# A decoder trunk in split fp32: the products with the weights' remainders moved to the end of each slab

## The chip, the cores and the metric

One Trainium2 chip, one core. The metric is the device time of one launch in microseconds (us). The core has TensorE (PE in the profile; its weight loads are PEld), VectorE (DVE), ScalarE (ACT), GpSimd (POOL) and the queue SP, which here starts the weight transfers.

## What is computed

The reference is one inference step of a two-layer hybrid decoder with 256 prompt tokens and 32 sample tokens (8 sequences of 4). All 288 tokens go through the kernel together.

```python
for l in range(DEPTH):                       # DEPTH = 2, D_MODEL = 2048, D_FF = 5632
    h = rms_norm(x, norm_mix[l])
    proj = h @ w_in[l]                       # 5120 columns
    q, k, v, hq, hf, hi, hg, cb, cc, ch = jnp.split(proj, split_idx, axis=-1)
    a = attention with sinks over a window of 128      # 16 query heads, 4 kv heads
    o = hgrn2_mixer(hq, hf, hi, hg, S0, lb, g_norm)    # 4 heads of 128
    yc = short_conv(cc * ch, buf, conv_w[l])
    x = x + jnp.concatenate([a, o, cb * yc], axis=-1) @ w_out[l]
    h = rms_norm(x, norm_ffn[l])
    gate, up = jnp.split(h @ w_gate_up[l], 2, axis=-1)
    x = x + (jax.nn.silu(gate) * up) @ w_down[l]
y = rms_norm(x, norm_final)
```

New caches and states are outputs too.

## The kernel before

Activations lie with the model dimension on the 128 partitions and the 288 tokens along the free axis. The five large matrices of a layer are one stream of slabs. A slab has 4 chunks of 128 input rows by 256 output columns (512 KB), and a layer has 376 slabs: 80 for the input projection, 16 and 16 for the two halves of the output projection, and for the feed-forward, in two parts of 24 and 20 tiles of its inner width, 96 and 48, then 80 and 40. Two layers have 752 slabs.

Every large product is done in fp32r three times, for accuracy: the weights are split into a rounded part `whi` and a remainder `wlo`, the activations into `xh` and `xl` (or `ah`/`al`, `mh`/`ml`, `fh`/`fl`). The sum has `whi*xh`, `whi*xl` and `wlo*xh`. A slab thus has 4 chunks x 2 column halves x 3 = 24 products of 128x128 by 128x288, each with its own weight load.

The engines work as a line, each on its own program, tied by semaphores:

- SP loads slab n into `raw` (ring of 4, L370) once the remainder of the slab four before is done.
- ScalarE rounds it, `whi <- raw` (L399), and counts `hi_ready`. It waits for `slab_used`, that is until TensorE is done with the slab four before.
- VectorE subtracts, `wlo = raw - whi` (L675), and counts `lo_ready`.
- TensorE (`group`, L1388) waits for `lo_ready`, does the 24 products and counts `slab_used` on the last.

ScalarE and VectorE call `hi` and `lo` two slabs ahead (`LEAD = 2`) of the slab that TensorE is to be at, in program order with their other work. The slabs of one pair of output tiles form a group (4 slabs in the projections into the layer, 2 in each half of the output projection, 6 or 5 in the down projection). Two pairs of PSUM banks alternate between groups. At a group's end VectorE empties the banks: `out_proj` (L707), `out_add` into `x` (L715), or `gb`/`fa` in the feed-forward (L1055, L1061), and counts `group_out`, for which TensorE waits before it uses the banks again.

In the second half of the output projection (`half_b`, a loop of 4 x 2 groups) each group also prepares the next norm's input. After `out_add` ScalarE makes `xh` (`scale_hi`, L406), then VectorE `xl` (`scale_lo`, L694), and GpSimd adds squares. After the first feed-forward group TensorE makes the mean square (L1437, L1438), ScalarE the root (L412), VectorE the reciprocal (L700), and only then VectorE can write `gb` and ScalarE its sigmoid (L572); ScalarE's next `whi` stands behind it. At the very start of the program ScalarE squares `x` between its first `whi` (L601), in step with GpSimd's sums (L1332).

The mixers' small products are woven in between as "fills", a generator that TensorE advances by one step: in the HGRN2 heads twice a slab (after the first column half and at the end of the slab), in the attention stretches once, at the end of the slab.

Of the kernel before, what the change touches and what calls it, by code (L numbers as in the profile page):

```python
# [29 lines left out]
P = 128  # L30
# [5 lines left out]
TOK = SEQ + SAMP  # L36
# [16 lines left out]
SLAB_K, SLAB_N = 4, 256  # L53
FF_TILES = D_FF // P
FF_PART = (24, 20)
RING = 4
# [60 lines left out]
def build(nc, wstream, x_in, consts, params, conv_buf, kt_cache, v_cache, caches, s_cache,  # L117
          y_out, kp_out, vp_out, ks_out, vs_out, caches_out, hp_out, hs_out, cv_out):
    ctx = ExitStack()
    with ctx:  # L120
        def sem(name):
            return ctx.enter_context(nc.semaphore(name))
# [9 lines left out]
        def sb(name, shape, dt=F32):  # L132
            t = nc.alloc_sbuf_tensor_at(name, shape, dt, offset=place[0])
            place[0] += size(shape)
            assert place[0] <= nc.sbuf_usable_end, (name, place[0], nc.sbuf_usable_end)
            return t
# [8 lines left out]
        def sub(where, name, shape, dt=F32):  # L145
            t = nc.alloc_sbuf_tensor_at(name, shape, dt, offset=where[0])
            where[0] += size(shape)
            assert where[0] <= where[1], name
            return t
# [19 lines left out]
        whi = [sb(f"whi{i}", [P, SLAB_K, SLAB_N], F32R) for i in range(RING)]  # L169
        wlo = [sb(f"wlo{i}", [P, SLAB_K, SLAB_N], F32R) for i in range(RING)]  # L170
# [22 lines left out]
        t = list(temp)  # L193
# [8 lines left out]
        t, u = list(temp), list(tail)  # L202
# [17 lines left out]
        s0 = sub(t, "s0", [P, DEC_BATCH, P])  # L220
# [3 lines left out]
        t, u = list(temp), list(tail)  # L224
# [21 lines left out]
        gp = [ctx.enter_context(nc.psum_tensor(f"gp{i}", [P, 512], F32)) for i in range(4)]  # L246
# [37 lines left out]
        hi_ready = sem("hi_ready")  # L284
        lo_ready = sem("lo_ready")
        slab_used = sem("slab_used")
# [1096 lines left out]
        def _(t):  # L1383
# [4 lines left out]
            def group(n4, s0, m, g, bank, mov, fill=None, halves=True):  # L1388


                t.wait_ge(group_out, g + 1)
                for s in range(m):
                    slot = (s0 + s) % RING
                    mov(s)
                    t.wait_ge(lo_ready, n4 * RING + (s0 + s + 1 + RING))
                    for c in range(2):
                        out = gp[2 * bank + c][:, 0:TOK]
                        for k in range(SLAB_K):
                            w_hi = whi[slot][:, k, c * P:(c + 1) * P]
                            w_lo = wlo[slot][:, k, c * P:(c + 1) * P]  # L1400
                            mv_hi, mv_lo = mov(s, k)
                            first, last = s == 0 and k == 0, s == m - 1 and k == SLAB_K - 1
                            t.matmul(out, w_hi, mv_hi, start=first, stop=False)  # L1403
                            t.matmul(out, w_hi, mv_lo, start=False, stop=False)  # L1404
                            mm = t.matmul(out, w_lo, mv_hi, start=False, stop=last)  # L1405
                        if c == 1:
                            mm.then_inc(slab_used, 1)
                        if fill is not None and (halves or c == 1):
                            next(fill, None)

            def from_x(tn):
                def mov(s, k=None):
# [224 lines left out]
            for l in range(DEPTH):  # L1637
                n4 = l * (SLABS // RING)
                g = l * GROUPS
                xin = from_x(l * 2)  # L1640
                if l == 0:
                    def late():
                        yield
                        yield
                        mean_square(0)
                        yield
                    group(n4, 0, 4, g, 0, xin)
                    group(n4, 4, 4, g + 1, 1, xin, late(), halves=False)
                else:
                    group(n4, 0, 4, g, 0, xin)  # L1650
                    mean_square(l * 2)
                    group(n4, 4, 4, g + 1, 1, xin)
# [4 lines left out]
                with t.Fori(0, HG_HEADS) as h:  # L1657
                    fill = hgrn(l * HG_HEADS + h, h, l)
# [4 lines left out]
                fill = attn(l * 2, 0, l)  # L1663
# [22 lines left out]
                fill = attn(l * 2 + 1, 1, l)  # L1686
# [12 lines left out]
                for part in range(2):  # L1699
# [9 lines left out]
                    k = FF_PART[part] // SLAB_K  # L1709
# [149 lines left out]
```

## Time and profile before

| | us |
|---|---|
| median of three runs | 2668.82 |
| lowest, highest | 2667.95, 2668.92 |
| profiled execution | 2661.78 |
| its span from first to last instruction | 2659.7 |

| engine | busy us | share of the span |
|---|---|---|
| PE | 2618.0 | 98% |
| PEld | 2572.8 | 97% |
| DVE | 1489.2 | 56% |
| ACT | 1003.5 | 38% |
| POOL | 352.9 | 13% |

Matmuls are pipelined: one starts while the one before is still in the array, so a product lasts about 0.3 us in the trace while starts are closer together. The step from start to start is what tells the pace of TensorE. The mean granted clock of the span is 0.993 of full speed.

### The profile page before, as it was taken

To read this page: it belongs to the slowest core of one execution; us is meant where nothing else is said; L and a number is where in the kernel's file an instruction comes from. 1 tells how busy PE (TensorE), PEld (TensorE's weight loads), DVE (VectorE), ACT (ScalarE), POOL (GpSimd) and SP (SyncE) were. 2 spreads that over 40 slices of the span, in tenths; PEclk is the share of its full clock that TensorE was granted. 3 is DMA by queue.
4 is the path that set the end of the run, shared out by engine and by line. 5 is a ranking of instruction groups with operands and counts; after the bars stand their busy time and mean duration, and the time that the engine had idled before them with its cause. 6 is when DMAs were issued, how large, how long until landed. Compare 5 with 4: busy or idle time off the path is not lost.

```text
span 2659.7 us, 51571 instructions
## 1 busy us (share of the span) xinstructions
PE 2618.0 (98%) x19472; PEld 2572.8 (97%) x19472; DVE 1489.2 (56%) x2051; ACT 1003.5 (38%) x1361; POOL 352.9 (13%) x299
## 2 busy tenths in 40 slices
PE   8999999999999999999999999999999999999997
PEld 8999899999999999999999999999999999999997
DVE  5566776655554445555555766875555544555555
ACT  5343443433333333333333434434333333333333
POOL 2001112211110011111100110131111100111111
PEclk9999999999999999999999999999999999999998
DMA  6444434444455444445444434345445454454443
GB/s 223 158 140 153 139 107 150 164 168 158 159 169 172 161 159 158 169 165 171 158 163 154 159 136 134 120 142 174 158 165 167 167 170 155 161 168 165 170 163 122
DMA packets 115723, 419.97 MB, mean 158 GB/s; under 512 B 13376, under 2 KB 14656, under 8 KB 115584
## 3 DMA queue, kind: packets, MB, share of 16 engines
q1 hardware_dynamic: 109152, 397.72, 44.6%
q0 software_dynamic: 3472, 14.04, 1.5%
q10 hardware_dynamic: 3024, 7.16, 0.7%
q8 instruction: 52, 0.85, 0.1%
q14 instruction: 23, 0.19, 0.0%
HBM read 411.06 MB, written 11.87 MB: 159 GB/s over the span
## 4 chain that ended last, share of the span: by engine, by line
PE 95%; DVE 3%; issue 1%; ACT 1%; POOL 1%; DMA 0%; DVEq 0%; SPq 0%; ACTq 0%; POOLq 0%
PE gp L1403 30%; PE gp L1405 29%; PE gp L1404 29%; PE mb L1447 1%; DVE wlo L675 1%; DVE qg L926 1%; PE mb L1518 1%; PE mb L1551 1%; PE mb L1606 0%; PE mb L1563 0%; POOL acc L1332 0%; PE mb L1550 0%; DVE rope_sin L916 0%; PE mb L1507 0%; PE mb L1456 0%
## 5 line engine op out<-in xcount | busy, mean ns | idle before, releaser
L1403 PE MATMUL gp<-xh,whi 128*128 128x288 f32 x4096 | 1227.2, 300 | 13.0 <-DVE xl L1097 9.6
L1404 PE MATMUL gp<-xl,whi 128*128 128x288 f32 x4096 | 1211.8, 296 | 0.0
L1405 PE MATMUL gp<-xh,wlo 128*128 128x288 f32 x4096 | 1207.9, 295 | 0.0
L675 DVE TENSOR_TENSOR wlo<-raw,whi 128x1024 fp32r<-128x1024 f32 x754 | 968.4, 1318 | 354.8 <-ACT whi L399 351.1
L399 ACT ACTIVATE whi<-raw 128x1024 fp32r<-128x1024 f32 x754 | 769.3, 1052 | 594.4 <-PE gp L1405 576.2
L1403 PEld LDWEIGHTS gp<-xh,whi 128*128 128x128 f32 x4096 | 771.2, 188 | 29.6 <-issue 28.1
L1405 PEld LDWEIGHTS gp<-xh,wlo 128*128 128x128 f32 x4096 | 774.6, 189 | 0.0
L1404 PEld LDWEIGHTS gp<-xl,whi 128*128 128x128 f32 x4096 | 772.7, 189 | 0.4
L1403 PE MATMUL gp<-fh,whi 128*128 128x288 f32 x1408 | 416.7, 296 | 0.0
L1404 PE MATMUL gp<-fl,whi 128*128 128x288 f32 x1408 | 415.4, 295 | 0.0
L1405 PE MATMUL gp<-fh,wlo 128*128 128x288 f32 x1408 | 414.0, 294 | 0.0
L1405 PEld LDWEIGHTS gp<-fh,wlo 128*128 128x128 f32 x1408 | 265.2, 188 | 0.0
L1404 PEld LDWEIGHTS gp<-fl,whi 128*128 128x128 f32 x1408 | 264.4, 188 | 0.0
L1403 PEld LDWEIGHTS gp<-fh,whi 128*128 128x128 f32 x1408 | 263.8, 187 | 0.0
L1363 POOL TENSOR_TENSOR gw<-gb,gs 128x576 f32<-128x576 f32 x44 | 63.2, 1436 | 1246.6 <-ACT gs L572 1246.6
L576 ACT ACTIVATE fh<-fa 128x576 f32 (+1 forms) x44 | 30.2, 686 | 284.9 <-DVE fa L1061 284.9
L1061 DVE TENSOR_TENSOR fa<-gp,gw 128x288 f32<-128x288 f32 x88 | 36.2, 452 | 177.8 <-PE gp L1405 177.8
L1055 DVE TENSOR_TENSOR gb<-gp,rstd 128x288 f32<-128x288 f32 x88 | 36.2, 452 | 171.7 <-PE gp L1405 171.4
L715 DVE TENSOR_TENSOR x<-gp,x 128x288 f32 (+1 forms) x128 | 52.3, 449 | 138.5 <-PE gp L1405 138.5
L572 ACT ACTIVATE gs<-gb 128x576 f32<-128x576 f32 x44 | 30.2, 687 | 263.6 <-DVE gb L1055 263.6
L1365 POOL TENSOR_TENSOR gw<-gw,rstd 128x576 f32<-128x576 f32 x44 | 100.9, 2294 | 3.4
L694 DVE SCALAR_TENSOR_TENSOR xl<-x,par,xh x64 | 69.5, 1126 | 46.9 <-ACT xh L406 46.9
(243 smaller groups left out, 1955.9 us busy)
## 6 DMA issues: line engine op xcount, KB each, us to landing
raw<-wstream SPq DMA_DIRECT2D x754, 512.0 KB, 4.1
s<-s_cache POOLq DMA_DIRECT2D x8, 512.0 KB, 9.7
hs_out<-s ACTq DMA_DIRECT2D x8, 512.0 KB, 2.8
caches_out<-caches POOLq DMA_DIRECT2D x8, 496.0 KB, 7.7
x<-x_in ACTq DMA_DIRECT2D x4, 576.0 KB, 8.6
y_out<-x SPq DMA_DIRECT2D x4, 576.0 KB, 2.8
kct<-kt_cache POOLq DMA_DIRECT2D x4, 512.0 KB, 3.7
vct<-v_cache POOLq DMA_DIRECT2D x4, 512.0 KB, 4.7
```

The source lines that it names most:

```text
L399: a.activation(whi[slot][:], raw[slot][:], ACT.Copy).then_inc(hi_ready, 1)
L572: a.activation(gs[:], gb[:], ACT.Sigmoid).then_inc(sig_ready, 1)
L675: v.tensor_tensor(wlo[slot][:], raw[slot][:], whi[slot][:].bitcast(F32), ALU.subtract).then_inc(lo_ready, 1)
L694: m = v.scalar_tensor_tensor(xl[:, xc, :], x[:, xc, :], pcol(P_GAIN, tn * KC + 2 * j + c), xh[:, xc, :].bitcast(F32), ALU.mult, ALU.subtract)
L715: m = v.tensor_tensor(xc, gp[2 * bank + c][:, 0:TOK], xc, ALU.add)
L1055: m = v.tensor_tensor(gb[:, c, :], gp[c][:, 0:TOK], rstd[:], ALU.mult)
L1061: m = v.tensor_tensor(fa[:, c, :], gp[2 + c][:, 0:TOK], gw[:, c, :], ALU.mult)
L1363: e.tensor_tensor(gw[:], gb[:], gs[:], ALU.mult).then_inc(gw_steps, 1)
L1365: e.tensor_tensor(gw[:], gw[:], rstd[:].unsqueeze(1).to_broadcast([P, 2, TOK]), ALU.mult).then_inc(gw_steps, 1)
L1403: t.matmul(out, w_hi, mv_hi, start=first, stop=False)
L1404: t.matmul(out, w_hi, mv_lo, start=False, stop=False)
L1405: mm = t.matmul(out, w_lo, mv_hi, start=False, stop=last)
```

## The change

In `group` the slab's 24 products are reordered. Before, each chunk had its three products in a row and the wait for `lo_ready` stood ahead of the slab. After, TensorE waits for `hi_ready` (ScalarE's count), does the sixteen products with `whi`, then waits for `lo_ready` and does the eight with `wlo`. `slab_used` is still counted on the last product of the slab. The fill after the first column half stands after 8 products instead of 12; the fill at the slab's end stays there.

```diff
                     mov(s)
+                    t.wait_ge(hi_ready, n4 * RING + (s0 + s + 1))
+                    for c in range(2):
+                        for k in range(SLAB_K):
+                            w_hi = whi[slot][:, k, c * P:(c + 1) * P]
+                            mv_hi, mv_lo = mov(s, k)
+                            t.matmul(gp[2 * bank + c][:, 0:TOK], w_hi, mv_hi, start=(s == 0 and k == 0), stop=False)
+                            t.matmul(gp[2 * bank + c][:, 0:TOK], w_hi, mv_lo, start=False, stop=False)
+                        if c == 0 and fill is not None and halves:
+                            next(fill, None)
                     t.wait_ge(lo_ready, n4 * RING + (s0 + s + 1 + RING))
                     for c in range(2):
-                        out = gp[2 * bank + c][:, 0:TOK]
                         for k in range(SLAB_K):
-                            w_hi = whi[slot][:, k, c * P:(c + 1) * P]
-                            w_lo = wlo[slot][:, k, c * P:(c + 1) * P]
-                            mv_hi, mv_lo = mov(s, k)
-                            first, last = s == 0 and k == 0, s == m - 1 and k == SLAB_K - 1
-                            t.matmul(out, w_hi, mv_hi, start=first, stop=False)
-                            t.matmul(out, w_hi, mv_lo, start=False, stop=False)
-                            mm = t.matmul(out, w_lo, mv_hi, start=False, stop=last)
-                        if c == 1:
-                            mm.then_inc(slab_used, 1)
-                        if fill is not None and (halves or c == 1):
-                            next(fill, None)
+                            mm = t.matmul(gp[2 * bank + c][:, 0:TOK], wlo[slot][:, k, c * P:(c + 1) * P], mov(s, k)[0],
+                                          start=False, stop=(s == m - 1 and k == SLAB_K - 1))
+                    mm.then_inc(slab_used, 1)
+                    if fill is not None:
+                        next(fill, None)
```

First place: TensorE in the second half of the output projection, the end of one slab and the start of the next. `ah` and `al` are the activations, `whi_72`/`wlo_76` and `whi_73`/`wlo_77` the two slabs' ring buffers. Before:

```order
L1403 MATMUL gp<-ah,whi_72 128x288
L1404 MATMUL gp<-al,whi_72 128x288
L1405 MATMUL gp<-ah,wlo_76 128x288
L1395 REGISTER_ALU [waits attn_vector]
L1403 MATMUL gp<-ah,whi_73 128x288 [waits lo_ready]
L1404 MATMUL gp<-al,whi_73 128x288
L1405 MATMUL gp<-ah,wlo_77 128x288
```

The same place after the change:

```order
L1400 MATMUL gp<-ah,whi_72 128x288
L1401 MATMUL gp<-al,whi_72 128x288
L1404 REGISTER_ALU
L1407 MATMUL gp<-ah,wlo_76 128x288 [waits lo_ready]
L1407 MATMUL gp<-ah,wlo_76 128x288 x7
L1395 REGISTER_ALU [waits attn_vector]
L1400 MATMUL gp<-ah,whi_73 128x288 [waits hi_ready]
L1401 MATMUL gp<-al,whi_73 128x288
```

The slab begins behind `hi_ready`, and `lo_ready` stands before its last eight products, with one register instruction ahead of it.

Second place: TensorE in an HGRN2 head, the step in the middle of the seventh slab, which computes the head's output (`AT`, `vk`, `s_112` are the mixer's tiles). Before, it stands after 12 products:

```order
L1404 MATMUL gp<-xl,whi_74 128x288
L1405 MATMUL gp<-xh,wlo_78 128x288
L1511 REGISTER_ALU
L1512 ISA [waits hgrn_scalar]
L1513 MATMUL mb<-AT,vk 128x256 [waits hgrn_state_loaded]
L1514 MATMUL mb<-AT,vk 128x128
L1515 MATMUL mb<-ATs,vks 128x32
L1518 MATMUL mb<-qk,s_112 128x4 x8
L1403 MATMUL gp<-xh,whi_74 128x288
```

After the change, it stands after 8:

```order
L1401 MATMUL gp<-xl,whi_74 128x288
L1513 REGISTER_ALU
L1514 ISA [waits hgrn_scalar]
L1515 MATMUL mb<-AT,vk 128x256 [waits hgrn_state_loaded]
L1516 MATMUL mb<-AT,vk 128x128
L1517 MATMUL mb<-ATs,vks 128x32
L1520 MATMUL mb<-qk,s_112 128x4 x8
L1400 MATMUL gp<-xh,whi_74 128x288
```

The step itself is the same; 4 fewer large products stand ahead of it in the slab, and 16 behind it instead of 12. On the other engines and the DMA queue no instruction moves.

## Rows read from the trace of the kernel before

**Rows 1.** The page: busy time of TensorE, and the chain of waits by line.

```profile
PE 2618.0 (98%) x19472; PEld 2572.8 (97%) x19472; DVE 1489.2 (56%) x2051; ACT 1003.5 (38%) x1361; POOL 352.9 (13%) x299
...
PE gp L1403 30%; PE gp L1405 29%; PE gp L1404 29%; PE mb L1447 1%; DVE wlo L675 1%; DVE qg L926 1%; PE mb L1518 1%; PE mb L1551 1%; PE mb L1606 0%; PE mb L1563 0%; POOL acc L1332 0%; PE mb L1550 0%; DVE rope_sin L916 0%; PE mb L1507 0%; PE mb L1456 0%
```

**Rows 2.** Stretches, products into gp alone: length, busy (count), clock, DMA share, GB/s.

```profile
505.00:1000.00 495.00, 495.00 (x3715) 1.00 0.49 164
600.00:640.00 40.00, 40.00 (x302) 1.00 0.47 157
450.00:490.00 40.00, 39.90 (x292) 1.00 0.49 158
1763.54:1803.54 40.00, 39.88 (x292) 1.00 0.49 159
600.00:610.00 10.00, 10.00 (x77) 1.00 0.59 185
495.00:505.00 10.00, 9.43 (x71) 1.00 0.17 59
1808.54:1818.54 10.00, 9.43 (x71) 1.00 0.19 61
```

**Rows 3.** Timeline of TensorE over a slab boundary: start, length, engine, line, tiles.

```profile
1003.81 0.29 PE L1405 MATMUL gp<-xh,wlo 128*128 128x288 f32 x1
1003.94 0.29 PE L1403 MATMUL gp<-xh,whi 128*128 128x288 f32 x1
```

**Rows 4.** Waits of TensorE on VectorE's remainders: total us, times, longest.

```profile
PE gp L1403 <- DVE wlo L675: 2.9, 5, 0.8
```

**Rows 5.** Timeline, the program's start: TensorE's stops, and VectorE.

```profile
28.97 0.38 PE L1403 MATMUL gp<-xh,whi 128*128 128x288 f32 x1 [0.77 <-DVE wlo L675]
...
41.20 0.39 PE L1403 MATMUL gp<-xh,whi 128*128 128x288 f32 x1 [0.43 <-DVE pj L707]
...
31.80 5.86 DVE L675 TENSOR_TENSOR wlo<-raw,whi 128x1024 fp32r<-128x1024 f32 x4 [2.98 <-ACT whi L399]
38.15 1.95 DVE L700 RECIPROCAL rstd<-rootx 128x288 f32<-128x288 f32 x1 [0.49 <-ACT rootx L412]
```

**Rows 6.** Timeline, second half of the output projection: VectorE, ScalarE, TensorE.

```profile
452.35 2.35 DVE L675 TENSOR_TENSOR wlo<-raw,whi 128x1024 fp32r<-128x1024 f32 x2
...
456.88 2.22 DVE L694 SCALAR_TENSOR_TENSOR xl<-x,par,xh  x2 [1.46 <-ACT xh L406]
459.03 2.34 DVE L675 TENSOR_TENSOR wlo<-raw,whi 128x1024 fp32r<-128x1024 f32 x2
...
456.62 2.00 ACT L399 ACTIVATE whi<-raw 128x1024 fp32r<-128x1024 f32 x2
...
459.98 0.29 PE L1405 MATMUL gp<-ah,wlo 128*128 128x288 f32 x1
460.29 0.40 PE L1403 MATMUL gp<-ah,whi 128*128 128x288 f32 x1
460.53 0.30 PE L1404 MATMUL gp<-al,whi 128*128 128x288 f32 x1
```

**Rows 7.** Timeline, the opening of the feed-forward part: VectorE, TensorE.

```profile
499.72 6.26 DVE L675 TENSOR_TENSOR wlo<-raw,whi 128x1024 fp32r<-128x1024 f32 x4 [1.70 <-ACT whi L399]
...
500.62 0.29 PE L1405 MATMUL gp<-xh,wlo 128*128 128x288 f32 x1
501.49 0.38 PE L1403 MATMUL gp<-xh,whi 128*128 128x288 f32 x1 [0.57 <-DVE wlo L675]
```

**Rows 8.** Timeline, second HGRN2 head of layer 0: VectorE and TensorE.

```profile
166.19 0.41 DVE L794 TENSOR_TENSOR AT<-mb,cst 128x256 f32<-128x256 f32 x1
...
169.17 0.61 PE L1447 MATMUL mb<-qk 128*128 128x128 f32 x4
```

**Rows 9.** Stretches in which the clock had fallen (first and last of seven), as rows 2.

```profile
263.00:266.50 3.50, 2.68 (x12) 0.52 0.07 11
1724.10:1727.50 3.40, 3.40 (x16) 0.51 0.16 64
```

## The prediction

> **What bounds the kernel now.** I read the page first: TensorE is busy in 98% of the span and holds 88% of the chain of waits by the three product lines alone; the line of VectorE's remainders (L675) has 1% of the chain [rows 1]. So time can only come out of places where TensorE doesn't issue its next product, and the question is how long those places are.
>
> Second, the stretches. In 495 us of feed-forward work TensorE starts 3715 products [rows 2], one per 0.133 us, and between a slab's last product and the next slab's first the step is the same (1003.81 to 1003.94, though the first product of a slab sits behind two semaphore waits) [rows 3]. That fixes two things: a wait whose semaphore is already up costs nothing, and in these 495 us VectorE's wait never holds TensorE. The 752 slabs of 24 products are 18048 x 0.133 = 2405 us; the other 255 us are the small products of the mixers, the start and the end, and a few real stops.
>
> Third, who makes TensorE stop. The view of waits puts only 2.9 us, five times, on VectorE's remainders [rows 4]. It understates: a stop shorter than the modelled end of the product before shows no idle time. Counting products in equal windows is better, because it counts lost steps. Against 302 in an undisturbed 40 us there are 292 in the 40 us around the end of the second half of the output projection, in layer 0 and in layer 1; against 77 in 10 us there are 71 around the seventh slab of the feed-forward part, again in both layers [rows 2].
>
> **The change, part by part.** Removed: nothing. Each slab still has 24 weight loads and 24 products, so the work is 2405 us as before. Added: one semaphore wait per slab, 752 in all, plus at most one register instruction in front of it. Moved: the wait for VectorE stands 16 products later (16 x 0.133 = 2.1 us); a filler step of the HGRN2 head that stood after product 12 stands after product 8; nothing moves on the other four engines or the DMA queue.
>
> *The added waits.* Priced at nothing while VectorE is early: [rows 3] show two satisfied waits for nothing. If that cover is gone (the wait drains what TensorE has fetched ahead), the price is what a real stop costs beyond its length: after the stop at 460.29 the second product comes at 460.53, 0.24 us later instead of 0.133 [rows 6], so 0.107 us per slab, 80 us in all. Bounds: 0 and 80 us. I take 0, because the nearest row, a boundary with satisfied waits, shows 0.
>
> The Trainium skill, page "TensorE: Matmul & The Clock Gate", section "Step-by-step: what each phase is for", says that TensorE pulls the next weight load ahead of products in flight, while the products keep their order. If a wait in the middle of a slab ended this pull-ahead, the rule would speak against the change, by the 80 us above; the trace's step at a slab boundary shows it surviving two waits.
>
> *The second half of the output projection (and the first feed-forward slabs).* Here VectorE and ScalarE form a loop of their own. Per group of two slabs VectorE makes two remainders and adds the result, waits 1.46 us for ScalarE's scaled xh, makes xl (2.22 us), and begins again: 452.35, then 459.03, i.e. 6.68 us [rows 6]. TensorE needs 48 x 0.133 = 6.39 us. It catches up with the loop and then stops at each group: 459.98 to 460.29, with 0.107 more behind it. The windows say 10 lost products per layer, 10 x 0.133 = 1.33 us, twice. After the change the remainder is wanted 2.1 us later. TensorE then runs ahead of the loop by what it loses today, 1.33 us by the end of the stretch, and stays inside 2.1 us. What is late next? ScalarE's rounded weights: they are started at 456.62, the first is ready about 457.7, and wanted at 460.0 [rows 6]; 2.3 us of room, 1.0 left after the gain. So the whole 1.33 us comes out: 2 x 1.33 = 2.7 us.
>
> *The feed-forward opening.* ScalarE resumes its rounded weights only after the mean square, root and first sigmoid. VectorE's x4 burst starts at 499.72, so the first rounded weight is ready by then; a remainder takes 6.26/4 = 1.6 us, so the first is there at 501.3. TensorE's next product was due at 500.62 + 0.13 and comes at 501.49 [rows 7]. After the change it needs only the rounded weight, which is ready 1 us before it gets there, and the remainder at 502.9. The windows say 6 lost products per layer: 0.80 us, twice 0.80 = 1.6 us. The pacing chain (mean square, root, reciprocal, sigmoid) starts from TensorE's own mean square, so it moves ahead with it.
>
> *The start.* Before 28.97 TensorE is idle for 0.77 us, and it stops at three more boundaries like this one, so at most 4 x 0.77 = 3.1 us [rows 5]. Most of this isn't to be had. The next result must pass VectorE, which works off four remainders from 31.80 to 37.66 without a pause, then makes the reciprocal at 38.15 after 0.49 us idle; TensorE waits for the projection behind it until 41.20 [rows 5]. An earlier TensorE saves the 0.49 us and no more; the rest of the stop moves to the group's wait at 41.2. Bounds 0 and 3.1; I take 0.5.
>
> *The filler steps.* In each of eight heads four steps come 4 products (0.53 us) earlier. The tightest that I find needs the copy that VectorE starts at 166.19 and ends at 166.60; TensorE arrives at 169.17, afterwards at 168.6: 2 us of room [rows 8]. Nothing gained, nothing lost: the same small products are still between the same large ones.
>
> Sum: 2.7 + 1.6 + 0.5 = 4.8 us. The profiled execution took 2661.8 us (2.1 more than its span), so it would take 2657.0. The three timed runs have their median at 2668.8, 7 us above the profiled one; I subtract from the median: **2664.0 us, 0.18% less**. What a measurement of this kernel can tell from no change is 0.2%, 5.3 us; the forecast lies just inside it.
>
> **The rivals.**
>
> *The stall only moves.* What holds at the start (gain swallowed by the next wait on VectorE) holds at the other two places: the feed-forward's stop turns into a wait for the group's bank or for xl, the loop of the projection hands its lateness on. For it: VectorE's loop is truly slower than TensorE there (6.68 against 6.39). Against: the lateness is handed to feed-forward slabs, where VectorE makes four remainders in a row (the 1.2 us remainders of a 3.2 us slab). Gain 0 to 2 us: 2667 to 2669. Chance 0.17.
>
> *The clock.* The granted clock falls to half seven times, from 263.1 to 1724.1; a fall lasts 3.4 us and 16 products start in it [rows 9] where 3.4 / 0.133 + 2 = 27.5 would, 1.5 us lost. The change shifts the mixers' steps by 0.5 us against each other and everything by up to 5 us, so one or two falls may come or go, by chance and not by merit. Two fewer, or more waits of this kind in the timed runs than in the profiled one (the 7 us are unexplained): 2659 to 2662, chance 0.15. Two more: 2667 to 2670, chance 0.05.
>
> *The wait in the middle costs.* This is the case on the other side: each of the 752 added waits stops the fetching ahead of weight loads. At full price 80 us: 2664 + 80 = 2744. It cancels the gain from 4.8 / 752 = 0.006 us per slab and makes the kernel slower by 0.2% from (4.8 + 5.3) / 752 = 0.013 us. For it: between the filler and the wait in a head only eight products hide it. Against: [rows 3]. Chance 0.04. With the small cases of two more falls about half reaching beyond no change, slower has 0.05.
>
> **How the numbers follow.** Forecast case 0.59, its own range 2662 to 2666: 0.5 gained at the start could be 0, the windows count to one product (0.13 us) in four windows, and the three times lie a microsecond apart. A gain of 5.3 us lies inside this range, so 0.4 of the case counts as faster: 0.24. With 0.15 from the clock: faster 0.39. Same: 0.35 + 0.17 + 0.04 = 0.56. Slower 0.05. The range from 2659.5 to 2668.5 leaves out the costly wait, the worst of the clock and the edge of no gain: about 2 in 10.
>
> **What the profile after would show.** The windows 450 to 490 and 495 to 505, shifted by the half microsecond of the start, hold 302 and 77 products in both layers; no step of 0.24 us follows a group boundary there. At the start TensorE stops less at the slabs and longer (about 1.5 us) just before its first product of the third group, near 40.7. Between the last rounded and the first remainder product of a slab the step is 0.133 us; if it is above 0.14 in steady stretches, the rival of the costly wait is on. The count of falls to half clock, seven before, tells how much of a difference is luck. The prediction would be wrong if the projection's windows still lack products, or if waits on the rounded weights (L399) appear in front of slabs.

## The result

The changed kernel takes 2676.13 us, the median of 14 runs (2671.12 to 2681.62). The kernel before, now with 14 runs, has 2668.06 (2663.42 to 2672.16). The ratio is 1.0033, with a 95% interval from 1.0025 to 1.0041: the change makes the kernel slower by a third of a per cent. The forecast was 2664.0, with a range from 2659.5 to 2668.5.

The profiled execution of the changed kernel took 2681.62 us; its span is 2679.6 us at a mean granted clock of 0.986. The page, busy time and chain (rows 1 of before):

```profile
PE 2638.1 (98%) x19472; PEld 2595.7 (97%) x19472; DVE 1489.1 (56%) x2051; ACT 1003.0 (37%) x1361; POOL 353.9 (13%) x299
...
PE gp L1400 30%; PE gp L1407 29%; PE gp L1401 29%; PE mb L1449 1%; PE mb L1520 1%; PE mb L1608 1%; DVE qg L926 1%; PE mb L1553 1%; PE mb L1565 0%; POOL acc L1332 0%; PE mb L1552 0%; DVE wlo L675 0%; DVE rope_sin L916 0%; PE mb L1458 0%; PE mb L1509 0%
```

The wait for VectorE's remainder has gone from the chain (1% to 0%), as meant, and still TensorE is busy 20.1 us longer with the same 19472 products [rows 1]. So the same products take longer. There are two sources, and the stretches show the first: length, busy time and count of products into `gp`, clock, DMA share, GB/s. After:

```profile
505.00:1000.00 495.00, 495.00 (x3704) 1.00 0.49 163
459.60:499.60 40.00, 40.00 (x302) 1.00 0.51 158
1782.20:1822.20 40.00, 40.00 (x302) 1.00 0.50 160
503.30:513.30 10.00, 10.00 (x77) 1.00 0.29 96
1826.70:1836.70 10.00, 10.00 (x77) 1.00 0.27 101
590.00:710.00 120.00, 120.00 (x898) 1.00 0.49 165
820.00:940.00 120.00, 120.00 (x902) 1.00 0.52 166
```

The last two stretches of the kernel before, which were not shown above:

```profile
590.00:710.00 120.00, 120.00 (x902) 1.00 0.50 166
820.00:940.00 120.00, 120.00 (x902) 1.00 0.50 164
```

Both stops are filled: 302 products where the windows at the same work (9.6 and 18.7 us earlier) had 292, and 77 where they had 71 [rows 2]. But 495 undisturbed microseconds hold 3704 products instead of 3715 [rows 2], and the loss sits in one kind of work. From 590 to 710 us TensorE multiplies by `xh` and `xl` (gate and up), 898 products instead of 902. From 820 to 940 it multiplies by `fh` and `fl` (down), and there nothing is lost. Measured from a slab's first product to the next slab's, an `xh` slab takes 3.213 us instead of 3.200 and an `fh` slab 3.200 as before, at full clock and with no wait. These are the medians over the slabs that hold no small product and no fall of the clock, 420 with `xh` and 175 with `fh`. The timeline of TensorE in the changed kernel, one slab (start, length, engine, line, tiles):

```profile
701.87 0.30 PE L1400 MATMUL gp<-xh,whi 128*128 128x288 f32 x1
702.01 0.30 PE L1401 MATMUL gp<-xl,whi 128*128 128x288 f32 x1
...
704.01 1.24 PE L1407 MATMUL gp<-xh,wlo 128*128 128x288 f32 x8
705.09 0.30 PE L1400 MATMUL gp<-xh,whi 128*128 128x288 f32 x1
```

Sixteen steps in 2.14 us and eight in 1.08, on average 0.134 and 0.135 us: no gap at the wait.

Is the slower slab a matter of what the other engines do at the time? The trace of the changed kernel answers it. Here are two of its `xh` slabs, each from its first product to the next slab's (length; busy time and count of TensorE, its weight loads, VectorE, ScalarE and GpSimd; clock, DMA share, GB/s):

```profile
692.23:695.45 3.22, 3.22 (x27) 3.22 (x26) 0.00 (x0) 0.00 (x0) 0.00 (x0) 1.00 0.82 290
698.66:701.87 3.21, 3.21 (x26) 3.21 (x25) 3.21 (x3) 1.64 (x2) 0.00 (x0) 1.00 0.31 96
```

In the first VectorE and ScalarE stand still, in the second VectorE writes remainders throughout; both slabs are equally slow. Over the 190 `xh` slabs without small products between 505 and 1400 us it is the same: the median is 3.213 us for the 48 in which VectorE makes no remainder and for the 43 in which it makes them all the time, with DMA shares from 0.03 to 0.98.

The second source is the clock. At 436.0 us the changed kernel has a fall to half clock where the kernel before has none, first after, then before:

```profile
436.00:439.50 3.50, 3.50 (x15) 0.52 0.02 5
```

```profile
427.80:431.30 3.50, 3.40 (x25) 1.00 0.03 6
```

The slab there takes 4.80 us instead of 3.29, so 1.5 us for about 3.4 us at half clock (0.44 us for each), as [rows 9] had it. The profiled execution of after has 14 falls, four of them twice as long, together 18 times 3.4 us at half clock; that of before had seven. These are extremes of both: over all runs the mean clock is 0.9903 before (27 runs beside e1 to e4) and 0.9878 after (14 runs). Time at half clock is twice the missing clock times the span, so 0.001 of mean clock is worth 2 x 0.001 x 2664 x 0.44 = 2.35 us, and the difference 5.9 us. The runs bear the price out: within one kernel their times fall by 2.3 us per 0.001 of mean clock (156 runs of 17 kernels).

That makes the account. The stops give 4.2 us: from the second slab of the output projection's second half to the eighth of the feed-forward part TensorE takes 71.5 us instead of 73.6, in both layers. The start gives some 0.6 (see the part on the prediction). 512 slabs with `xh` at 13.3 ns more cost 6.8; the 32 slabs with `mh`, which also lie at an odd multiple, would cost 0.4 at the same price, but small products stand in them and their step can't be read. The clock costs 5.9. The sum is +8.3 us; the means differ by 8.8. Without the clock's part it is +2.4, where the table below has 2.9 ± 0.5.

### The profile page after: what moved, and what is told of

Same layout as the page of the kernel before. It is cut to its first block, busy times and chain, and to the rows that moved or that the text cites. A ratio compares the mean times of both kernels' runs of the same rounds, so it can differ in the third digit from the quotient of the medians.

```text
span 2679.6 us, 52151 instructions
## 1 busy us (share of the span) xinstructions
PE 2638.1 (98%) x19472; PEld 2595.7 (97%) x19472; DVE 1489.1 (56%) x2051; ACT 1003.0 (37%) x1361; POOL 353.9 (13%) x299
## 4 chain that ended last, share of the span: by engine, by line
PE 96%; DVE 2%; issue 1%; POOL 1%; ACT 0%; DMA 0%; DVEq 0%; SPq 0%; ACTq 0%; POOLq 0%
PE gp L1400 30%; PE gp L1407 29%; PE gp L1401 29%; PE mb L1449 1%; PE mb L1520 1%; PE mb L1608 1%; DVE qg L926 1%; PE mb L1553 1%; PE mb L1565 0%; POOL acc L1332 0%; PE mb L1552 0%; DVE wlo L675 0%; DVE rope_sin L916 0%; PE mb L1458 0%; PE mb L1509 0%
## 5 line engine op out<-in xcount | busy, mean ns | idle before, releaser
L1400 PE MATMUL gp<-xh,whi 128*128 128x288 f32 x4096 | 1129.3, 300 | 12.3 <-DVE xl L1097 9.9
L1401 PE MATMUL gp<-xl,whi 128*128 128x288 f32 x4096 | 1115.9, 298 | 0.0
L1407 PE MATMUL gp<-xh,wlo 128*128 128x288 f32 x4096 | 638.3, 298 | 0.0
L1407 PEld LDWEIGHTS gp<-xh,wlo 128*128 128x128 f32 x4096 | 585.9, 190 | 0.0
L1401 PE MATMUL gp<-fl,whi 128*128 128x288 f32 x1408 | 380.8, 295 | 0.0
L1400 PE MATMUL gp<-fh,whi 128*128 128x288 f32 x1408 | 380.6, 298 | 0.0
L1407 PE MATMUL gp<-fh,wlo 128*128 128x288 f32 x1408 | 216.3, 296 | 0.0
L1407 PEld LDWEIGHTS gp<-fh,wlo 128*128 128x128 f32 x1408 | 196.3, 188 | 0.0
```

What stands on the lines that cost most here:

```text
L1400: t.matmul(gp[2 * bank + c][:, 0:TOK], w_hi, mv_hi, start=(s == 0 and k == 0), stop=False)
L1401: t.matmul(gp[2 * bank + c][:, 0:TOK], w_hi, mv_lo, start=False, stop=False)
L1407: mm = t.matmul(gp[2 * bank + c][:, 0:TOK], wlo[slot][:, k, c * P:(c + 1) * P], mov(s, k)[0], start=False, stop=(s == m - 1 and k == SLAB_ ...
```

## The experiments

Each ran beside the kernel before, whose median was between 2666.9 and 2668.1 us each time. The table splits each difference of means into the clock's part, 2.35 us per 0.001 of mean clock, and the rest (with its 95% interval). "Step" is the time of a slab with `xh` and of one with `fh` in its profile. Four executions of 5 to 13 ms (one each in e6, e9, e10, e16) are left out, their cause is not known; that of e9 was its profiled one.

| kernel | median us (runs) | ratio to before (95%) | clock's part | rest | step xh / fh, ns |
|---|---|---|---|---|---|
| before | | | | | 3200 / 3200 |
| after | 2676.1 (14) | 1.0033 (1.0025-1.0041) | +5.9 | +2.9 ± 0.5 | 3213 / 3200 |
| e1 | 2681.7 (5) | 1.0056 (1.0042-1.0070) | +6.8 | +6.7 ± 0.4 | 3213 / 3200 |
| e2 | 2668.8 (11) | 1.0008 (0.9999-1.0017) | +0.9 | +0.3 ± 0.5 | 3200 / 3200 |
| e3 | 2667.0 (11) | 1.0002 (0.9993-1.0011) | +1.8 | -1.5 ± 0.6 | 3200 / 3213 |
| e4 | 2665.6 (11) | 0.9990 (0.9981-0.9999) | +2.2 | -4.7 ± 0.5 | 3200 / 3200 |
| e5 | 2665.8 (11) | 0.9995 (0.9986-1.0004) | +3.5 | -5.2 ± 0.6 | 3200 / 3200 |
| e6 | 2675.5 (5) | 1.0028 (1.0015-1.0040) | +4.9 | +2.0 ± 1.1 | 3213 / 3200 |
| e7 | 2667.6 (12) | 1.0008 (0.9997-1.0019) | +0.9 | +1.2 ± 0.5 | 3200 / 3200 |
| e8 | 2668.6 (11) | 1.0004 (0.9996-1.0013) | +5.6 | -4.5 ± 0.6 | 3200 / 3200 |
| e9 | 2667.9 (11) | 0.9999 (0.9990-1.0008) | +1.3 | -1.1 ± 0.6 | not read |
| e10 | 2667.3 (11) | 0.9995 (0.9986-1.0004) | +4.9 | -6.0 ± 0.5 | 3200 / 3200 |
| e12 | 2669.0 (11) | 1.0012 (1.0002-1.0021) | +1.3 | +1.2 ± 0.5 | 3200 / 3200 |
| e13 | 2659.3 (11) | 0.9976 (0.9968-0.9985) | +8.2 | -15.1 ± 0.6 | 3177 / 3200 |
| e14 | 2650.8 (5) | 0.9942 (0.9929-0.9955) | +2.3 | -17.7 ± 0.8 | 3173 / 3173 |
| e15 | 2652.4 (6) | 0.9960 (0.9946-0.9974) | +5.3 | -16.7 ± 1.0 | 3177 / 3187 |
| e16 | 2675.6 (5) | 1.0033 (1.0021-1.0046) | +6.5 | +2.5 ± 0.6 | 3213 / 3200 |
| e17 | 2646.2 (5) | 0.9917 (0.9904-0.9931) | +1.7 | -23.2 ± 0.9 | 3173 / 3173 |

e11 and e18 have one run each: 2656.3 us with 3177 / 3200, and 2670.7 us with 3200 / 3227. The 3177 of e11, e13 and e15 is a mean: about half of these slabs take 3173 ns and half 3180.

**Is it the wait or the order?** e1 has the new order, with the one wait for `lo_ready` back at the slab's start. e2 has the old order and one more wait, whose semaphore is up, between the column halves.

```diff
 # e1, against after
-                    t.wait_ge(hi_ready, n4 * RING + (s0 + s + 1))
+                    t.wait_ge(lo_ready, n4 * RING + (s0 + s + 1 + RING))
...
-                    t.wait_ge(lo_ready, n4 * RING + (s0 + s + 1 + RING))
 # e2, against before
                     for c in range(2):
+                        if c == 1:
+                            t.wait_ge(hi_ready, n4 * RING + (s0 + s + 1))
```

> The changed order of the 24 products, but with VectorE's wait at the slab's start as before, and no second wait. The profile after the change showed a slab of 3.213 us instead of 3.200 us wherever the moving operands are xh and xl, and 3.200 us with fh/fl or ah/al. Theory A (the order makes it: a weight load of wlo now runs while a product of wlo streams xh): slabs with xh/xl take 3.213 us here too, the stops in the second half of the output projection are back, so 2668 + 6.8 + about 2 = 2675 to 2680 us. Theory B (the wait in the middle makes it): slabs take 3.200 us everywhere and the time is that of before, 2668 +- 2 us.

> The order of before, with one more semaphore wait (on ScalarE's count, always up by then) between the two column halves of every slab. Theory B (a satisfied wait in the middle costs 13 ns in slabs with xh/xl): 3.213 us per slab there and about 2675 us. Theory A (the order): 3.200 us everywhere and the time of before.

e1, the stretch with `xh`, the one with `fh`, and the one of the stops:

```profile
590.00:710.00 120.00, 120.00 (x898) 1.00 0.48 161
820.00:940.00 120.00, 120.00 (x902) 1.00 0.50 165
450.00:490.00 40.00, 39.97 (x292) 1.00 0.49 158
```

e2, the same 495 us as in [rows 2]:

```profile
505.00:1000.00 495.00, 495.00 (x3715) 1.00 0.49 165
```

The order alone slows the `xh` slabs. At equal clock it costs 6.7 ± 0.4 us, as 512 x 13.3 ns would, and without the later wait the gain at the stops is missing: the stretch from 450 to 490 us holds 292 products as before (after has a rest of +2.9). A satisfied wait in the middle of a slab costs nothing: 3715 products as before, +0.3 ± 0.5 us. The rival of the costly wait falls.

**Why xh and not fh?** The two differ in where they lie. In SBUF, the on-chip memory with the activations and the ring, `xh` begins 89216 bytes ahead of `wlo`, 697 x 128; `fh` begins 16384 behind it, 128 x 128. e3 puts the ring ahead of `x`, which makes `xh` an even and `fh` an odd number of 128 bytes away from it. e5 puts `xh` 128 bytes on and the ring 256, so that their distance changes by 128. e6, the control, puts `xh` and everything behind it, the ring too, 256 bytes on: the addresses change, the distance doesn't.

```diff
 # e3, against after: raw, whi, wlo allocated here, not behind rstd
+        raw = [sb(f"raw{i}", [P, SLAB_K, SLAB_N]) for i in range(RING)]
+        whi = [sb(f"whi{i}", [P, SLAB_K, SLAB_N], F32R) for i in range(RING)]
+        wlo = [sb(f"wlo{i}", [P, SLAB_K, SLAB_N], F32R) for i in range(RING)]
         x = sb("x", [P, KC, TOK])
 # e5, against after (e6: 256, and nothing before rstd)
+        place[0] += 128
         xh = sb("xh", [P, KC, TOK], F32R)
...
+        place[0] += 128
         rstd = sb("rstd", [P, TOK])
```

> The changed kernel with the weight ring (raw, whi, wlo) placed ahead of x, xh and xl in the memory instead of behind them; nothing else differs. If the 13 ns per slab come from where xh and wlo lie relative to each other (theory A, by address), the slabs with xh/xl or those with fh/fl change their time, 3.213 to 3.200 us or the other way; a gain of up to 6.8 us on the changed kernel, or a loss of 3 us. If the wait or the order alone make it, xh slabs stay at 3.213 us and fh slabs at 3.200 us.

> The changed kernel with xh, xl, mh and ml moved 128 bytes further in each partition against the weight ring (the ring itself moves by 256). Over the kernels so far a slab takes 3.213 us where the offset between its moving operand and wlo is an odd multiple of 128 bytes, and 3.200 us where it is a multiple of 256 (xh, mh odd and fh, ah even in the changed kernel; the other way round with the ring first). By that rule all slabs take 3.200 us here, 6.8 us come back on the fast slabs and a little more in the mixers: 2676.1 - 7.5 = 2668.6 us, and down to 2664 us if the extra clock falls go with it, as they did with the ring first. If only the region of the memory matters (ahead of or behind the ring), nothing changes: 3.213 us and 2676 us.

> Control: the changed kernel with xh and everything behind it moved by 256 bytes; the offset between xh and wlo stays as in the changed kernel. The 128-byte rule says 3.213 us with xh/xl and 3.200 us with fh/fl as after the change, about 2676 us. If any shift would do, xh slabs come down.

e3, stretches as above, `xh` first:

```profile
590.00:710.00 120.00, 120.00 (x903) 1.00 0.47 161
820.00:940.00 120.00, 120.00 (x898) 1.00 0.50 164
```

e5, then e6:

```profile
590.00:710.00 120.00, 120.00 (x903) 1.00 0.49 165
820.00:940.00 120.00, 120.00 (x903) 1.00 0.51 166
```

```profile
590.00:710.00 120.00, 120.00 (x899) 1.00 0.47 157
820.00:940.00 120.00, 120.00 (x902) 1.00 0.52 166
```

The slow steps have changed sides with the placement: 903 and 898, where after has 898 and 902. With the distance changed by 128 bytes (e5) both are at 3200; with all moved together (e6) `xh` stays slow. The tile, its stage and the engines beside it are the same in all of these, so the slow step belongs to the distance between activations and ring. "Odd" and "even" stand here for where the areas begin. A chunk of 288 tokens has 1152 bytes, 9 x 128, so from chunk to chunk of a slab the distance is odd and even by turns in either case; why the one turn is slower than the other these runs don't show. e5 is the changed kernel without its loss: -5.2 ± 0.6 us at equal clock, about what the prediction expected of the change, and 3.5 us of it are given back by a lower clock.

**The gain alone.** e4 uses the new order only where TensorE stops: in the second half of the output projection and in the first two feed-forward groups of a layer. e10 is e4 with the 128 bytes of e5.

```diff
 # e4, against before; `if late:` chooses after's order in group
-            def group(n4, s0, m, g, bank, mov, fill=None, halves=True):
+            def group(n4, s0, m, g, bank, mov, fill=None, halves=True, late=False):
...
-                        group(n4 + i, 2 * b, 2, g + i * 2 + b, b, from_mix(ah, al, half_b))
+                        group(n4 + i, 2 * b, 2, g + i * 2 + b, b, from_mix(ah, al, half_b), late=True)
```

> The changed order with its two waits only in the groups in which TensorE stopped for VectorE: the second half of the output projection and the first two groups of the feed-forward part of each layer; everywhere else the program of before. The prediction's gains there (2.7 + 1.6 us) should come without the cost elsewhere: 2668 - 4.3 + 0.2 = 2664 us, 0.15% below before. If the slower time comes from clock falls that any shift of the program makes, it is as likely 2666 to 2672.

> The changed order only in the second half of the output projection and the first two feed-forward groups, with the offset of 128 bytes. The stops gone as in the run without the offset, and the few xh slabs at 3.200 us: at equal clock 2647.5 us + 1.5 per fall. With 11.6 falls 2665 us, with 13.9 falls 2668.5 us. If the offset draws the falls the second, if not the first.

e4, the stretches of both layers in which before had 292 products:

```profile
450.00:490.00 40.00, 40.00 (x302) 1.00 0.49 162
1763.54:1803.54 40.00, 40.00 (x302) 1.00 0.51 162
```

The stops are worth 4.7 ± 0.5 us at equal clock (the trace has 4.2 us in the two stretches named above, 71.5 us instead of 73.6 in both layers); the clock takes 2.2 of it.

Two rests have no step to explain them: with 128 bytes e9 is 1.1 us ahead of before and e10 1.3 ahead of e4, although all of these have 3200 / 3200 where it was read. They are little more than their intervals, and their cause is open.

**Where do the clock falls come from?** Until the last large product the clock falls, in every profile but the disturbed one of e9, only in slabs in which the mixers run or in the first slab behind them. e7 has the new order only in groups with fills, e8 only in groups without (and 128 bytes), e9 is before with 128 bytes, and e12 is before with twelve more products ahead of layer 0's feed-forward, which moves layer 1 by 1.6 us.

```diff
 # e7, against before (e8: is None), with e4's choice in group
+                late = fill is not None
 # e12, against before
+                if l == 0:
+                    for _ in range(12):
+                        t.matmul(mb[2][:, 0:TOK], xh[:, 0, 0:P], xh[:, 1, :], start=True, stop=True)
```

> The changed order only in groups that carry filler steps (heads, attention, first output half: 72 of 376 slabs a layer), the order of before elsewhere; placement as before. If the four extra clock falls per run come from the mixers' stretches with the changed order, the mean clock is about 0.988 as after the change, and the time 2667.5 + 6 (falls) + 2 (slower slabs with xh/mh) = 2675 us. If they don't, the clock is 0.990 and the time about 2670 us.

> The changed order in all groups without filler steps, the order of before in those with them, and the offset of 128 bytes. All slabs at 3.200 us, the stops gone: 2667.5 - 4.8 = 2662.7 us if the falls are as before (clock 0.990). This should be the fastest of all; if it has the extra falls, 2668 us.

> The kernel before, with xh, xl, mh and ml moved 128 bytes against the weight ring, nothing else. Slabs take 3.200 us at either offset with the order of before (theory: only the changed order is sensitive), so 2667.5 us as before. If the offset itself draws clock falls (it went with 12.5 and 13.9 falls a run in the last two kernels that had it, against 10.2 before), the mean clock is about 0.988 and the time 2671 to 2673 us.

> The kernel before with twelve extra products (into a free bank, result unused) between the output projection and the feed-forward part of layer 0, which moves all of layer 1 later by 12 x 0.133 = 1.6 us. If the number of clock falls is a matter of how the stretches lie in time, the falls of layer 1 change against those of layer 0 and the clock leaves 0.990 (time 2666 to 2673 us). If each place draws falls by what it holds, the clock stays at 0.990 and the time is 2667.5 + 1.6 = 2669 us.

The order in the mixers isn't what lowers the clock: e7 has it and loses 0.9 us (its median is below both of its expectations, though its runs spread widest, 2663.6 to 2678.8 us), e8 and e10 don't have it there and lose 5.6 and 4.9, as much as after. Moving layer 1 (e12) or the tiles (e9) loses 1.3 each. No edit sorts the kernels into those with many falls and those with few. Every kernel with five runs or more had a somewhat lower mean clock than before, which may be chance: before may be a lucky arrangement. The cause of the falls stays open. e7's rest, 1.2 ± 0.5 us, is not more than the slow steps can explain (e7 has the new order in 100 `xh` and 32 `mh` slabs, 132 x 13.3 ns = 1.8 us), so moving the fills costs nothing that shows.

**How far does the placement go?** e11 puts `xh` 64 bytes on (and 192 before `rstd`, so that the ring moves by 256); e13 is the same kernel, timed. e14 is the kernel before and e15 the changed one with all activations off by 64: e11's edit and one more ahead of `fh` and `ah`. e16 moves `x` and all behind it by 64, so that no distance changes. e17 is e4 with e14's placement, e18 before with 32 instead of 64.

```diff
 # e11, against after
+        place[0] += 64
         xh = sb("xh", [P, KC, TOK], F32R)
...
+        place[0] += 192
         rstd = sb("rstd", [P, TOK])
 # e14 (against before), e15 (against after): as e11, and
+        place[0] += 64
         wide = area(2 * max(FF_PART) * TOK * 4)
```

> The changed kernel with the activations moved by 64 bytes against the ring instead of 128. If whole steps of 256 bytes set the pairing, 64 lies between: a slab of 3.200 or 3.213 us, or a third value, tells which boundary counts. Profile only.

> The kernel of e11 again, timed. Placement and order together: 512 slabs at 3.178 instead of 3.213 us are 18 us, and with the attention's slabs some 20: 2656 to 2658, ratio 0.996 of before. If e11's single 2656 was a lucky number of clock falls: 2659 to 2662. If it was a disturbance: 2665 or more.

> The kernel before with all activations (xh, xl, mh, ml, fh, fl, ah, al) 64 bytes off the ring modulo 128, order unchanged. If the placement works only where products with whi stand sixteen in a row: slabs 3200 ns as before, 2666 to 2669. If placement alone gives it: slabs at 3178 or less in all stretches, 16 us less, 2650 to 2653.

> The kernel after with the same placement as e14. If the 22 ns per slab come from order and a distance of 64 modulo 128 together, also the 208 slabs with fh, fl, ah, al go to 3178: e13 less 4.6 us, 2651 to 2653, and it beats both kernels by 0.6%. If the gain belongs to xh and xl alone: 2656 as e13.

> The kernel after with x and everything behind it moved on by 64 bytes, so that no distance between activations and ring changes. If the distance decides: xh slabs 3213, fh slabs 3200, 2675 to 2677 as after. If the address itself decides: xh slabs at another time, 3178 or 3200.

> The placement of e14 with the late order only where TensorE stops (e4). If the two gains are independent: e14's 2650.8 less the 4.6 us of the stops, 2646 to 2648, the fastest of all, unless clock falls come on top as in e10 (4 more, 6 us: 2651 to 2653). If stops and steps share their time: 2650 to 2652.

> The kernel before with all activations 32 bytes off the ring modulo 128 instead of 64. If only the distance of 64 counts: slabs 3200, span about 2662. If any distance that is no multiple of 128 counts, or the gain grows with it: slabs at 3173 or between 3173 and 3200.

Stretches as above, `xh` first, of e14:

```profile
590.00:710.00 120.00, 120.00 (x909) 1.00 0.49 165
820.00:940.00 120.00, 120.00 (x910) 1.00 0.51 165
```

Of e15, and under it of e18:

```profile
590.00:710.00 120.00, 120.00 (x909) 1.00 0.50 170
820.00:940.00 120.00, 120.00 (x906) 1.00 0.51 166
```

```profile
590.00:710.00 120.00, 120.00 (x903) 1.00 0.49 163
820.00:940.00 120.00, 120.00 (x894) 1.00 0.50 162
```

Of e16:

```profile
590.00:710.00 120.00, 120.00 (x898) 1.00 0.47 157
820.00:940.00 120.00, 120.00 (x903) 1.00 0.52 166
```

Four things follow. A distance of 64 bytes modulo 128 makes the step shorter than any before, in the old order too: 3173 ns against 3200, so the kernel before with three lines of padding takes 2650.8 us. I had rather expected the two to act together only (e14's first line); that was wrong. The distance decides, not the address: e16 is as slow as after, 898 and 903 products where after has 898 and 902. Nor does every distance off the multiples of 128 help: 32 bytes leave `xh` at 3200 and make `fh` slower, 3227. And the order still matters at the good distance (3173 old; new 3177 with `xh` and 3187 with `fh`). The distance of the areas doesn't settle everything: in e13 it is the second and fourth slab of a group that take 3180 ns, in e15 the first and third, though `xh` and the ring lie alike in both.

e17 joins the two gains: late waits only where TensorE stops, old order elsewhere, activations 64 bytes off. It takes 2646.2 us, 0.83% less than before (ratio 0.9917, 0.9904 to 0.9931), and is the fastest of all. e13 came out at 2659.3, above the 2656 to 2658 expected, because its mean clock is the lowest of all, 0.9871. e17's stretch in the second half of the output projection holds 304 products, where e14, which still stops there, holds 291; e17, then e14:

```profile
450.00:490.00 40.00, 40.00 (x304) 1.00 0.48 158
```

```profile
450.00:490.00 40.00, 39.70 (x291) 1.00 0.49 158
```

The gains add up: -17.7 for the placement and -4.7 for the stops are -22.4, measured -23.2 ± 0.9 at equal clock.

## Why the prediction was wrong

**The stops: right.** In the output projection the forecast was 302 products per 40 us; there are 302 in both layers. The feed-forward opening holds 77 per 10 us, as forecast. The forecast had 2.7 + 1.6 = 4.3 us for these two places; the traces of before and after have 4.2, and e4, which has the change only there, gains 4.7 ± 0.5. The loop of VectorE takes nearly as long as before, 6.59 us from one pair of remainders to the next in the changed kernel (VectorE's timeline: 448.78, then 455.37), but TensorE now stays within the lateness that it allows.

**The start: right, one bound too low.** The waits of TensorE in the changed kernel (total us, times, longest) and its timeline there:

```profile
PE gp L1400 <- ACT whi L399: 2.4, 3, 1.1
```

```profile
28.05 0.37 PE L1400 MATMUL gp<-xh,whi 128*128 128x288 f32 x1 [0.54 <-ACT whi L399]
32.26 0.37 PE L1400 MATMUL gp<-xh,whi 128*128 128x288 f32 x1 [0.79 <-ACT whi L399]
40.97 0.40 PE L1400 MATMUL gp<-xh,whi 128*128 128x288 f32 x1 [1.10 <-ACT whi L399]
```

The stop before the third group has grown from 0.43 to 1.10 us, and that group begins at 40.97 instead of 41.20 [rows 5]: 0.2 us gained, forecast 0.5. One pair of executions says little here, because they differ by as much when the order is the same. Over the profiles of all kernels but e9 the third group begins at 41.24 us on average where the remainders are waited for before the slab (10 profiles, 41.0 to 41.5) and at 40.67 where they are waited for after sixteen products (9 profiles, 40.0 to 41.1): some 0.6 us. The upper bound, 4 x 0.77 = 3.1 us, was too low: in the trace of before the fourth to the eighth slab take 3.59, 4.20, 4.20, 4.03 and 4.00 us, 4.0 us more than five slabs of 3.20. The waits for ScalarE's rounded weights, of which the prediction said that they would prove it wrong, did appear, but only here: three waits, 2.4 us in all, in place of those for the remainders made from the same weights.

**The added waits: right.** Priced at nothing between bounds of 0 and 80 us; e2 measures +0.3 ± 0.5 us, and no time is lost at the wait in after: the step across it is 0.136 us on average. The one behind it, from the first to the second product with `wlo`, is the longest of the slab, 0.145 us, but it is as long in e1, which has no wait there. So the price of a stop does not apply to a wait that is satisfied.

**The step that failed** is "Each slab still has 24 weight loads and 24 products, so the work is 2405 us as before", the term for the work, whose change was put at nothing. The count is right, the step of 0.133 us was taken as a constant of the product's shape. It is the step of the old order at this placement. In the new order it is 0.1339 us where the activations begin an odd multiple of 128 bytes from the ring: the 512 `xh` slabs of 752, 6.8 us, more than the whole gain of 4.8. The rival "the wait in the middle costs" had named two sizes, 0.006 us per slab from which the gain is gone and 0.013 from which the kernel is 0.2% slower; 0.0133 in two slabs of three is what was lost, by another mechanism: e1 loses it without the wait. The prediction bounded the price of the wait and gave the order none. That its rival came near the size that was measured is luck. On the Trainium skill's page "TensorE: Matmul & The Clock Gate", section "Step-by-step: what each phase is for", weight loads and the moving operand have read ports of their own, so that loading the next weights takes no read bandwidth from the product that runs. The runs here don't fit this as it stands: with the same instructions in the same order the slab takes 3200 or 3173 ns by the distance between activations and weights alone (before and e14). The measurement decides; whether it is the loads that slow the products, no run shows.

**The clock: right in kind, wrong in weight.** The case "two more falls, 2667 to 2670" had a chance of 0.05, and a change of the count was called chance. The mean over 14 runs is lower by 0.0025, worth 5.9 us; single runs spread (0.986 to 0.990 after, 0.989 to 0.992 before), but the means belong to the kernels. Its cause is open; in the prediction it is the chance of 0.05 that it speaks against. Without the clock's part the change still loses 2.9 us, so the clock doesn't make the sign. One open number of the prediction is also answered: the 7 us between before's profiled execution and its median are mostly clock, 0.993 against 0.9903, 2.7 x 2.35 = 6.3 us.

## What to carry to other kernels

Before the order of products is changed in a kernel that TensorE fills to 98%, price the step itself: 13 ns per slab of 24, 0.4% of it, outweighed two stops that were found and sized rightly (4.2 us, forecast 4.3). A count of products in long undisturbed stretches, per kind of operand, shows it in one look. Where a reordering must only help at a few places, do it at these places; and try the distance between the two operands of TensorE in SBUF, the on-chip memory that holds them (here 64 bytes modulo 128), since it cost three lines and gave more than the reordering.

## What was not expected of the hardware

- The step of back-to-back products (128x128 weights, 128x288 moving, fp32r) at full clock depends on the distance between the areas of the moving operand and of the weights, modulo 128 or 256 bytes. Old order: 3200 ns per slab at odd and at even multiples of 128, 3173 at 64, and at 32 bytes 3200 (`xh`) or 3227 (`fh`). New order: 3213 at odd, 3200 at even multiples, at 64 3177 (`xh`) or 3187 (`fh`). In the changed kernel an `xh` slab takes 3213 ns whether VectorE makes remainders all the time or not at all.
- Which part of the memory or of TensorE makes it so, no run here shows; only weights in the ring and activations in the areas named were moved, and `raw`, `whi` and `wlo` always together.
- Kernels with the same products differ in their mean clock by 0.003 (0.9871 in e13 to 0.9903), up to 8 us in the means over 5 to 27 runs each, with no cause found.
